# MLP of a decoder layer: the inner width in two parts, the second product in groups of two k tiles by 1024 columns, the residual kept in SBUF

## What is computed

```python
x = layer_norm(DEEPNORM_ALPHA * x + attn_out, ln1_g, ln1_b)
hdn = jnp.square(jax.nn.relu(jnp.einsum('bsd,df->bsf', x, w_ff1)))
ff_out = jnp.einsum('bsf,fd->bsd', hdn, w_ff2)
x = layer_norm(DEEPNORM_ALPHA * x + ff_out, ln2_g, ln2_b)
```

## Time and profile before

| | us |
|---|---|
| median of three runs | 1114.44 |
| lowest and highest | 1114.32, 1114.58 |
| span of the profiled execution | 1111.8 |
| TensorE busy in that span | 1099.9 |
| DVE busy, ACT busy | 660.4, 531.7 |

### The profile page before, as it was taken

The page is one execution under the profiler, slowest core; times in us unless marked ns, Lnnn a source line. Parts: engine busy times, 40 slices in busy tenths (PEclk is TensorE's granted clock), DMA queues, the critical chain, the costliest instruction groups (busy, mean ns, idle before and its releaser), DMA issues.

```text
span 1111.8 us, 15143 instructions
## 1 busy us (share of the span) xinstructions
PE 1099.9 (99%) x5660; PEld 933.3 (84%) x5660; DVE 660.4 (59%) x709; ACT 531.7 (48%) x684; POOL 29.9 (3%) x54
## 2 busy tenths in 40 slices
PE   9999999999999999999999999999999999999996
PEld 8888888888888888888888888888888888888885
DVE  6677758667556775655565556555445445445446
ACT  6577757555543434444444444444433343333431
POOL 1001001000000010000000000000000000000001
PEclk9999999999999999999999999999999999999998
DMA  9856564575546646566666666667555555555572
GB/s 298 264 183 211 185 186 153 173 244 172 172 168 210 226 152 208 177 196 192 190 177 199 190 190 178 196 192 264 191 194 197 194 189 192 196 198 188 191 270 89
DMA packets 126973, 217.77 MB, mean 196 GB/s; under 512 B 6913, under 2 KB 41985, under 8 KB 126289
## 3 DMA queue, kind: packets, MB, share of 16 engines
q1 hardware_dynamic: 125520, 209.74, 59.0%
q0 software_dynamic: 1408, 7.41, 1.9%
HBM read 212.93 MB, written 4.19 MB: 195 GB/s over the span
## 4 chain that ended last, share of the span: by engine, by line
PE 98%; DVE 1%; issue 0%; POOL 0%; POOLq 0%; ACT 0%; DVEq 0%
PE low_ps L510 11%; PE low_ps L636 11%; PE high_ps L407 10%; PE high_ps L405 10%; PE high_ps L403 10%; PE high_ps L636 9%; PE low_ps L515 6%; PE low_ps L403 5%; PE low_ps L641 5%; PE low_ps L407 5%; PE low_ps L405 5%; PE high_ps L641 5%; PE high_ps L450 1%; PE high_ps L477 1%; PE high_ps L461 0%; PE low_ps L380 0%
## 5 line engine op out<-in xcount | busy, mean ns | idle before, releaser
L930 DVE TENSOR_TENSOR w_lo<-w_raw,w_hi 128x1024 fp32r<-128x1024 f32 x372 | 454.7, 1224 | 389.6 <-ACT w_hi L702 388.5
L702 ACT ACTIVATE w_hi<-w_raw 128x1024 fp32r<-128x1024 f32 x372 | 394.0, 1060 | 496.7 <-PE high_ps L407 194.4
L403 PE MATMUL high_ps<-w_hi,hidT_hi 128*128 128x512 f32 x480 | 186.7, 389 | 0.0
L405 PE MATMUL high_ps<-w_lo,hidT_hi 128*128 128x512 f32 x480 | 186.7, 389 | 0.0
L407 PE MATMUL high_ps<-w_hi,hidT_lo 128*128 128x512 f32 x480 | 186.7, 389 | 0.0
L510 PE MATMUL low_ps<-xT,w_hi 128*128 128x512 f32 x512 | 179.4, 397 | 0.0
L636 PE MATMUL low_ps<-x1T,w_hi 128*128 128x512 f32 x512 | 176.7, 393 | 0.0
L636 PE MATMUL high_ps<-x1T,w_hi 128*128 128x512 f32 x448 | 155.0, 394 | 0.0
L515 PE MATMUL low_ps<-xT,w_lo 128*128 128x256 f32 x512 | 139.8, 283 | 0.0
L641 PE MATMUL low_ps<-x1T,w_lo 128*128 128x256 f32 x512 | 136.9, 278 | 0.0
L641 PE MATMUL high_ps<-x1T,w_lo 128*128 128x256 f32 x448 | 119.8, 278 | 0.0
(11 more groups left out here) (145 smaller groups left out, 957.9 us busy)
## 6 DMA issues: line engine op xcount, KB each, us to landing
w_raw<-in_w_ff SPq DMA_DIRECT2D x252, 512.0 KB, 3.7
w_raw<-in_w_in SPq DMA_DIRECT2D x92, 512.0 KB, 4.1
w_raw<-in_w_out SPq DMA_DIRECT2D x32, 512.0 KB, 3.6
x_raw<-in_x_turned SPq DMA_DIRECT2D x8, 256.0 KB, 6.0
w_raw<-in_w_in SPq DMA_DIRECT2D x8, 256.0 KB, 5.3
y<-in_x SPq DMA_DIRECT2D x8, 256.0 KB, 4.6
side_raw<-in_w_ff SPq DMA_DIRECT2D x4, 512.0 KB, 6.6
ln_spill<-y POOLq DMA_DIRECT2D x8, 256.0 KB, 2.8
```

The lines of the kernel that those rows point to most:

```text
L403: pe.matmul(acc[:, tt, 0:cols], hi[:, toks], right_hi[:, slot, w], start=(t == 0), stop=False)
L405: pe.matmul(acc[:, tt, 0:cols], hi[:, toks], right_lo[:, slot, w], start=False, stop=False)
L702: act.activation(w_hi[:, slot, :], w_raw[:, slot, :], ACT.Copy).then_inc(w_rounded, units)
L930: dve.tensor_tensor(w_lo[:, slot, :], w_raw[:, slot, :], w_hi[:, slot, :].bitcast(F32), ALU.subtract).then_inc(w_split, units)
```

## The change

- The inner width is cut in two parts, chunks 0 to 6 and 7 to 15 (`FF_PARTS`). The order becomes: ff1 of part 0, ff2 of part 0, ff1 of part 1, ff2 of part 1. Each ff2 has two passes, one for each half of 1024 output columns (`PASSES`). A pass sums in four banks (two token tiles by two times 512 columns).
- The unit of ff2 is a pair (`PAIRS`, 64 of them): two k tiles by 1024 columns, 128x2048 values, 1 MB in two transfers with rows of 4 KB, where a unit was 128x1024 values in one transfer with rows of 2 KB. A pair has 24 matmuls. There are three places for raw pairs (`PAIR_SLOT`) and two for the rounded and split ones.
- After the first three passes DVE adds the sums to `y1` (`add_pass`). `y1` stays in SBUF; `spill`, its eight writes, its read back and the wait of DVE for the writes are gone.
- At the end the last two pairs (`TAIL`) are done sum by sum: token tile 0, first and second 512 columns, then token tile 1. DVE adds them with `add_tail`.
- The hardware loops of the MLP are written out, and the region reserved for POOL's DMA descriptors is 4096 bytes a partition.
- The matmuls are the same in number, shape and operands' types.

```diff
+FF_PARTS = ((0, 7), (7, 16))
+PASSES = [(part, half) for part in range(2) for half in range(2)]
+PAIR_SLOT = [q % 3 if q < PART_END else (1, 0, 2)[(q - PART_END) % 3] for q in range(len(PAIRS))]
+TAIL = 2
-    spill = nc.dram_tensor("ln1_spill", [P, TT, D_MODEL], F32).ap()
...
+    def load_pair(sp, q):
...
+        if first < 2:
+            sp.wait_ge(w_split, U_FF1 + UPH * FF_PARTS[part][1] - 2 + 2 * first)
+        elif first == 2:
+            sp.wait_ge(w_used, U_FF1 + (UPH * CHUNKS_FF if part else UPH))
+        else:
+            sp.wait_ge(plain_split, q - 2)
+        for n in range(2):
+            sp.dma_start(pair_raw(q)[:, n * HALF:(n + 1) * HALF],
+                         w_ff2_d[:, t + n, half, :]).then_inc(pair_loaded[PAIR_SLOT[q]], 16)
...
+        for q in range(PART_END, len(PAIRS) - TAIL):
+            pair_group(q)
+        for tt in range(TT):
+            for half in range(2):
+                for q in range(len(PAIRS) - TAIL, len(PAIRS)):
+                    pe.wait_ge(plain_split, q + 1)
+                    for n in range(2):
+                        ins = plain_products(q, n, tt, half, False, q == len(PAIRS) - 1 and n == 1)
+                ins.then_inc(tail_done, 1)
...
+        def round_pair(q):
...
+            if q == len(PAIRS) - 1:
+                act.wait_ge(plain_used, PASS_END[0])
+            elif first < 2:
+                act.wait_ge(w_used, U_FF1 + UPH * FF_PARTS[part][1] - 2 + 2 * first)
+            else:
+                act.wait_ge(plain_used, q - 1)
+            act.activation(plain_home(q)[0], pair_raw(q), ACT.Copy).then_inc(plain_rounded, 1)
...
+        def add_pass(p):
...
+            for tt in range(TT):
+                mine = y1[:, tt, cols].rearrange("p (b n) -> p b n", b=2)
+                dve.scalar_tensor_tensor(out=mine, in0=mine, scalar=1.0 if part else ALPHA,
+                                         in1=sums_of(p)[:, 2 * tt:2 * tt + 2, :], op0=ALU.mult,
+                                         op1=ALU.add).then_inc(y2_summed, 1)
...
+        for q in range(PART_END + 4, len(PAIRS)):
+            split_pair(q)
+            if q == PASS_START[3]:
+                add_pass(2)
...
+            if tt == 0:
+                add_tail(0, 0, 2, 2, 1)
+                final_stats(0, 2)
+                final_stats(0, 3)
+            else:
+                add_tail(1, 1, 1, 4, 3)
+                final_stats(1, 3)
...
+                elif tt == 0:
+                    add_tail(1, 0, 1, 3, 2)
+                    final_stats(1, 2)
...
-        for i, (tt, c) in enumerate(PIECES):
-            pool.wait_ge(x1_ready, i + 1)
-            pool.dma_start(spill[:, tt, cols], y1[:, tt, cols]).then_inc(spilled, 16)
...
-        pool.dma_start(y2[:, :, :], spill).then_inc(x1_back, 16)
...
+                   dynamic_dma_scratch_size=4096)
```

More of the change, by code:

```diff
@@ L295, in load_chunk_unit @@
     def load_chunk_unit(sp, w, u, row, chunk, slot, back=SLOTS):
[L297 removed]
+        if u >= SLOTS:
             sp.wait_ge(w_split, u - (back - 1))
         dst = w_raw[:, slot, :].rearrange("p (k n) -> p k n", k=KU)
[L300 to L302 removed]
+        sp.dma_start(dst, w[:, row, :, chunk, :]).then_inc(w_loaded[slot], 16)
     def load_in_unit(sp, u):
@@ L627, in hidden_unit @@
             slot = k % SLOTS
-            for b in (2, 3, 0, 1) if second else range(TPC):
-                if k == 0 and second and b == 0:
+            for b in (2, 3, 0, 1) if i == 1 else range(TPC):
+                if k == 0 and i == 1 and b == 0:
                     pe.wait_ge(relu_done, TT)
@@ L1234, in vector_program @@
         square_first()
-        dve.wait_ge(spilled, 16 * len(PIECES))
-        for k in range(UPH):
-            if k == 2:
-                split_first_hidden()
-            ahead(UPH + U_FF1, k)
-        square_hidden(1, low_ps)
-        def hidden_chunk(i, banks):
-            for k in range(UPH):
-                if k == 1:
+        for i in range(1, FF_PARTS[0][1]):
+            for k in range(UPH if i < FF_PARTS[0][1] - 1 else UPH - SLOTS):
+                if i == 1 and k == 2:
+                    split_first_hidden()
+                if i > 1 and k == 1:
@@ new lines, in vector_program @@
+            if i < FF_PARTS[0][1] - 1:
+                square_hidden(i)
+        for q in range(3):
+            split_pair(q)
+        square_hidden(FF_PARTS[0][1] - 1)
+        split_pair(3)
+        split_pair(4)
+        split_hidden(FF_PARTS[0][1] - 1)
+        for q in range(5, PART_END):
+            split_pair(q)
+            if q == PASS_START[1]:
+                add_pass(0)
+        for n in range(FF1_PART, FF1_PART + 2):
+            split_late(n)
+        add_pass(1)
+        for n in range(FF1_PART + 2, FF1_PART + SLOTS):
+            split_late(n)
@@ new lines, in vector_program @@
+        for i in range(*FF_PARTS[1]):
+            for k in range(UPH if i < FF_PARTS[1][1] - 1 else UPH - SLOTS):
+                if i > FF_PARTS[1][0] and k == 1:
+                    split_hidden(i - 1)
+                split_late(UPH * i + k + SLOTS)
+            if i < FF_PARTS[1][1] - 1:
+                square_hidden(i)
+        split_pair(PART_END)
+        split_pair(PART_END + 1)
+        split_pair(PART_END + 2)
+        square_hidden(FF_PARTS[1][1] - 1)
+        split_pair(PART_END + 3)
```

386 lines of the change are left out of this document (218 added, 168 removed).

## The result

| | before | after |
|---|---|---|
| median of the runs beside each other | 1114.38 us (1114.05 to 1114.58, 4 runs) | 1121.02 us (1120.77 to 1121.53, 4 runs) |
| span of the profiled execution | 1111.8 us | 1119.7 us |
| ff2's matmul distance | 226.7 ns | 226.7 ns |
| hole at the first pairs of part 1 | none | 1.56 us |
| start of the last matmul to the end | 10.83 us | 15.07 us |

The ratio is 1.0059, with a 95% interval of 1.0045 to 1.0073: slower by 6.6 us, where 5.4 was forecast. 1121.02 lies inside the range.

A forecast was written before the change was run, and what follows sets the result against it. TensorE, busy for 1099.9 of 1111.8 us, was taken as the bound, plus the work after its last matmul. Terms 0 + 1.2 (hole) + 4.2 (end) = 5.4 us gave 1114.44 + 5.4 = 1119.8 us; range 1116.8 to 1122.0.

The forecast's parts named there:

- Matmuls, 0: All 1536 ff2 matmuls of 512 columns keep their distance of 226.7 ns despite the new order: no time change.
- the faster rival: New order of banks and stationary tiles shortens ff2's matmul distance; 5 ns less gives 1112.1 us, 13.4 gives 1099.2; chance 3%.
- Spill, 0: Dropping the eight writes, the read back and DVE's wait gains nothing, since TensorE has no hole there.
- Steady pairs, 0: In ff2, rounding and splitting a pair takes 4.68 us against 5.67 before TensorE wants it: no holes.
- `add_pass`, 0: DVE's additions after the first three ff2 passes delay a split by 0.4 us at most, within 0.5 of slack: no hole.
- Hole at pair 31, 1.2 us: From ff1 to ff2 of part 1, pair 31's rounding queues behind the hidden values': TensorE waits 1.2 us, 1.6 with upper durations.
- Slow spacing in ff1: Rival: written-out chunks 3 to 15 take chunk 2's 173.9 ns a matmul, not 170.9: 5.0 us more, 1124.8; chance 7%.
- End, +4.2 us: After the last matmul, DVE is still on tile 0, so tile 1's last addition starts late: end 4.2 us later.
- The alternative: At the end, POOL as quick for tile 0 as at tile 1 would make the added delay 0.6 us less.
- Pair 63's cover: In the tail, the last pair's split ends at 1.4 us and is wanted at 1.6: thin slack, no cost added.
- From the span to the runs: Timed runs lie 2.6 us above their span, so 5.4 us was added to 1114.44.

## Why the prediction held, point by point

- **Matmuls, 0: right.** From 907.36 to 1104.65 there are 864 matmuls; less the hole and the 0.06 of the tail that is 195.67 / 863 = 226.7 ns, the figure of before. The order of banks and stationary tiles was not what kept the distance above the ideal, so the faster rival had nothing to win. The Trainium skill (TensorE: Matmul & The Clock Gate, "Back-to-back issue gap") would have 215.8 ns by the rule that the prediction used, which it gives for an isolated matmul; for a stream of weight loads and matmuls it has about 131 ns. The trace agrees with neither: both kernels have 226.7.
- **Spill, 0: right**, and shown alone by the kernel without it.
- **Steady pairs, 0: right.** The extended durations were 1.92 and 2.29 us; the page of after has 1916 and 2291 ns. The Trainium skill (VectorE: DVE Perf Modes, "The TRN2 errata") gives (N + 151) / 0.96 ns for an addition of two fp32 operands, 2291 for 2048 columns, and the trace agrees for this subtraction. The one wait in the groups of L696 shows that no pair came late.
- **`add_pass`, 0: right.** No TensorE distance is above the usual at any of the three; the rest of the delay was taken by the cover, as worked out.
- **Hole at pair 31, 1.2 us: the mechanism right, the size 0.4 short** (1.56 and 1.59 in two profiles; the upper bound was 1.6, from another term). Of the 0.4, about 0.15 to 0.2 comes from pair 30's data: ACT started it 6.03 us after the start of ff1's last matmul (913.16 - 907.13), released by the transfer, where the prediction had the data at 5.4 and the start at 5.88. The landing was built from transfers of rows half as long. Another 0.15 lies between the end of DVE's split (925.02) and TensorE's start (925.17), and 0.08 in the second distance, 0.30 us instead of 0.227; the prediction let TensorE start the moment the split ended and at full pace.
- **Slow spacing in ff1: excluded.** The prediction divided 20 us by the counts of the earlier trace rows, which include matmuls that began before the window, and had 173.9 and 170.9 ns. From start to start chunk 2 has 176.5 and the others 173.4; the difference, and so the rival's 5 us, stays the same.
- **End, +4.2 us: right** (4.24; in all 15.07 us, where 14 to 15 were named). The prediction didn't divide it; the experiments with 24 matmuls in before and 36 in after do, 1.8 or 2.7 for the tail and 2.4 or 1.5 for DVE's added work. The alternative, that POOL answers sooner after the statistics, didn't occur: `finish_norm` began 3.01 us after `centre` (1102.59 to 1105.60), the same as in the earlier trace rows.
- **Pair 63's cover was called thin** (0.2 us) and costed at nothing; it cost 0.06.
- **From the span to the runs: wrong by 0.6 to 0.8.** The prediction added 5.4 to the median, which holds if the profile of before is typical. Its span was 2.6 us below the median; in the repeated kernels the time lies 2.0 us (before) and 1.8 us (after) above the span. The first profile of before had its first full unit at 16.8 us, the earliest of all. It doesn't change the sum, since both medians are of runs, but differences of single spans (1119.7 - 1111.8 = 7.9 us) overstate the change by over a microsecond.
- **Missing: some 0.7 us at the start.** No term stood for it. It is the rest of the 1.2 us between 5.4 and 6.6. About half goes with the loops being written out, which the prediction priced only as a risk for ff1's spacing; the cause is open.
- **Luck: a little.** Every miss (0.4 in the hole, 0.06 in the tail, 0.7 at the start) was on the slow side, and 1121.02 is inside the forecast's own bounds of 1118.4 to 1121.2 by 0.2 us only.

## What to carry to other kernels

When one engine is busy for 99% of the span, as here, saved traffic and saved instructions of the others are worth nothing that could be measured, and a change has to be read by what it does to that engine's holes and to the work behind its last instruction. Here the larger units with two places leave about 1 us of cover, so an instruction that waits for another engine (the rounding of the hidden values) must not stand ahead of a unit in the same program: move the unit ahead of it. And the length of the part that is done tile by tile at the end must cover all post-processing of the earlier tile, including every small instruction of the last tile that is put among it.

## What the runs showed of the hardware that I had not expected

- After a wait, TensorE's second distance is longer as well: 0.30 and 0.31 us behind the hole of pair 31, 0.34 behind the one in the tail of three pairs, where 0.227 is usual.
- POOL took 2.89 us for an instruction of 128x512 with two per-partition scalars, but 1.44 and 1.26 us for additions and multiplications of two tensors of the same size. The first ran beside a busy DVE, the second for a part, the third alone; how much of the 2.89 is that and how much the form was not separated.
- While POOL's first was under way, a DVE instruction of two tensors and 512 columns took 1.09 us, 0.34 more than its like in the repeated before. The others that overlapped it took 0.75, 0.49, 0.47 and, two in a row, 0.87 us, as their likes did in the repeated before, so not everything on DVE was slowed.
